# Replacing the per-block interleave of two work threads by one order over all blocks, in a hybrid SSM/RG-LRU decoder layer

## What is computed

```python
h = rms_norm(x, g_mix)
z = h @ w_in + b_in                       # 3584 columns: u_a 512, u_b 1024, two gates of 1024
y_a = s5_mixer(u_a, ...)                  # in projection, complex scan over L, out projection, gelu, GLU
y_b = rglru_mixer(u_b, ...)               # conv of width 4, two sigmoid gates, scan over L
merged = gate_a * (y_a @ w_a_out) + gate_b * (y_b @ w_b_out)
x = x + merged @ w_o
h2 = rms_norm(x, g_ffn)
x = x + (silu(h2 @ w_ffn_gate) * (h2 @ w_ffn_up)) @ w_ffn_down      # hidden 2816
gate_p = sigmoid(rms_norm(x, g_ple_gate) @ w_ple_gate + b_ple_gate)
x = x + gate_p * rms_norm(p @ w_ple, g_ple)
return rms_norm(x, g_final)
```

## Time and profile before

| what | us |
|---|---|
| median of 2 runs | 2377.64 (2377.08 to 2378.2) |
| the profiled execution's own time | 2382.28 |
| its span on the slowest core, 3 | 2380.6 |
| spans of the 8 cores | 2360.8 to 2380.6 |
| PE busy | 1295.1 (54%), 4896 matmuls |
| DVE busy | 1396.3 (59%) |
| ACT busy | 716.3 (30%) |
| chain that ended last | DVE 33%, PE 30%, issue 15%, ACT 12%, DMA 9% |

### The profile page before, as it was taken

How to read it: one execution, slowest core, us unless ns; L and a number is a source line. 1 busy time by engine, 2 the same in 40 slices (tenths; PEclk the granted TensorE clock), 3 DMA queues, 4 the chain that set the end, 5 groups by cost and what they waited for, 6 DMA issues and landing times.

```text
span 2380.6 us, 18703 instructions; the slowest of 8 cores (2360.8 to 2380.6 us)
## 1 busy us (share of the span) xinstructions
PE 1295.1 (54%) x4896; PEld 512.0 (22%) x4896; DVE 1396.3 (59%) x2787; ACT 716.3 (30%) x1085; POOL 143.0 (6%) x153
## 2 busy tenths in 40 slices
PE   0041111256666775356667765267567774388975
PEld 0020000022222321132222321132122221133431
DVE  2608787814777776525877775516777775433123
ACT  0152222061123334361123334351224234312114
POOL 1000000000000100000000100000000100001100
PEclk9995555578879986678879986678779976588987
DMA  9130000036645880435634960425725951348990
GB/s 179 26 72 0 0 0 0 8 80 86 81 58 69 87 108 18 85 79 84 91 51 62 103 92 18 111 57 80 106 36 78 100 79 38 78 62 132 126 106 36
DMA packets 211064, 164.42 MB, mean 69 GB/s; under 512 B 93712, under 2 KB 202896, under 8 KB 210704
## 3 DMA queue, kind: packets, MB, share of 16 engines
q0 software_dynamic: 200928, 132.13, 42.6%
q1 hardware_dynamic: 10032, 31.09, 3.9%
HBM read 286.94 MB, written 8.39 MB: 124 GB/s over the span
## 4 chain that ended last, share of the span: by engine, by line
DVE 33%; PE 30%; issue 15%; ACT 12%; DMA 9%; DVEq 1%; ACTq 0%; SPq 0%; POOL 0%; POOLq 0%
PE ps L452 18%; PE ps L761 4%; DMA slot<-w_b_out 3%; DVE tmp L593 2%; DVE tmp L594 2%; DVE tmp L573 2%; DVE tmp L571 2%; DVE tmp L569 2%; DVE tmp L540 1%; DMA out<-tmp 1%; PE ps L814 1%; DVE tmp L445 1%; DMA slot<-w_in 1%; DVE FB L447 1%; DMA x_fm<-iota 1%
## 5 line engine op out<-in xcount | busy, mean ns | idle before, releaser
L452 PE MATMUL ps<-FB,slot 128*128 128x512 bf16 x1920 | 498.8, 414 | 112.3 <-DVE hid L749 54.5
L452 PEld LDWEIGHTS ps<-FB,slot 128*128 128x128 bf16 x1920 | 196.6, 104 | 399.5 <-issue 218.2
L761 PE MATMUL ps<-hid,slot 128*128 128x512 bf16 x704 | 169.4, 401 | 14.2 <-DMA slot<-w_ffn_down 6.9
L528 PE MATMUL ps<-xcb,wr_sb 128*128 128x512 bf16 x32 | 16.6, 520 | 255.4 <-DVE xcb L525 255.4
L452 PE MATMUL ps<-hid,slot 128*128 128x512 bf16 x384 | 105.3, 423 | 72.2 <-DMA slot<-w_a_out 32.7
L486 PE MATMUL ps<-ident_bf,A 128*128 128x128 bf16 x128 | 16.2, 306 | 212.2 <-DVE small L475 123.8
L612 PE MATMUL ps<-sbf,Csb 128*32 128x512 bf16 x64 | 29.9, 467 | 175.1 <-DVE sbf L605 175.1
L749 DVE TENSOR_TENSOR hid<-tmp,ps 128x512 bf16<-128x512 f32 x88 | 58.8, 685 | 110.3 <-PE ps L452 96.7
L814 PE MATMUL ps<-slot,FB 128*128 128x512 bf16 x256 | 97.1, 523 | 40.7 <-ACT tmp L802 30.5
L445 DVE RECIPROCAL tmp<-tmp 128x512 f32<-128x512 f32 x12 | 40.2, 3353 | 105.8 <-ACT tmp L444 105.8
L452 PE MATMUL ps<-tmp,slot 128*128 128x512 bf16 x384 | 95.4, 413 | 11.4 <-DMA slot<-w_in 10.8
(11 more groups left out here) (203 smaller groups left out, 2421.1 us busy)
## 6 DMA issues: line engine op xcount, KB each, us to landing
slot<-w_in POOLq DMA_DIRECT2D x28, 1024.0 KB, 12.3
slot<-w_ffn_down POOLq DMA_DIRECT2D x32, 704.0 KB, 13.3
slot<-w_ffn_gate POOLq DMA_DIRECT2D x20, 1024.0 KB, 14.5
slot<-w_ffn_up POOLq DMA_DIRECT2D x20, 1024.0 KB, 10.8
tmp<-x SPq DMA_DIRECT2D x32, 512.0 KB, 4.6
slot<-w_b_out POOLq DMA_DIRECT2D x8, 1024.0 KB, 13.9
slot<-w_o POOLq DMA_DIRECT2D x8, 1024.0 KB, 16.0
slot<-w_ple_gate POOLq DMA_DIRECT2D x8, 1024.0 KB, 12.1
```

What stands on the lines that cost most here:

```text
L452: V("pe", lambda e, k=k: e.matmul(ps[:, bn, :], lhsT=slab_lhsT(si, cols, k, c0), rhs=rhs_fn(k), start=(k == 0), stop=(k == kt - 1)), [B_sl ...
L761: V("pe", lambda e, k=k, si=si, cols=cols, bn=bn: e.matmul(ps[:, bn, :], lhsT=slab_lhsT(si, cols, k, 0), rhs=hid[:, k * TB:(k + 1) * TB], ...
```

## The change

A single `schedule` takes two generators that run over all blocks: `S_all` emits S(0) to S(3) one after another, `F_all` emits F(0) to F(3), and F(b) gives way ("W") until S(b) is complete. The next step goes to the side whose position (block number plus the share of its total) is smaller; while the flag `ramp` is set, F and S take turns. The flag is set at the start of each S block and cleared when its RG-LRU and S5 parts begin. The conditions `merged` and `down` stay as they are. The number of steps, their instructions, the weights and the buffers are unchanged.

```diff
+                prog["ramp"] = False
                 gL, gS5 = LRU_gen(), S5_gen()
...
-            run_all(S_thread(0))
-            for b in range(NB):
-                if b + 1 < NB and PIPELINE:
-                    interleave(F_thread(b), S_thread(b + 1), 330.0, 430.0)
-                else:
+            def S_all():
+                for b in range(NB):
+                    prog["ramp"] = True
+                    yield from S_thread(b)
+                    prog["s_done"] = b
+                    prog["s_blk"] = b + 1
+
+            def F_all():
+                for b in range(NB):
+                    while prog["s_done"] < b:
+                        yield "W"
+                    prog["f_blk"] = b
+                    yield from F_thread(b)
+                prog["f_blk"] = NB
+
+            def schedule(gF, gS, totF, totS):
...
+                    if prog["f_blk"] != bF_seen:
+                        bF_seen, pF = prog["f_blk"], 0.0
+                    if prog["s_blk"] != bS_seen:
+                        bS_seen, pS = prog["s_blk"], 0.0
+                    posF = bF_seen + pF / totF
+                    posS = bS_seen - 1 + pS / totS
+                    if doneS or s_blocked:
+                        pickF = True
+                    elif doneF or f_blocked:
+                        pickF = False
+                    elif prog["ramp"]:
+                        turn ^= 1
+                        pickF = bool(turn)
+                    else:
+                        pickF = posF <= posS
...
+            prog.update({"s_done": -1, "s_blk": 0, "f_blk": 0, "ramp": True})
+            if PIPELINE:
+                schedule(F_all(), S_all(), 330.0, 430.0)
```

More of the change, by code:

```diff
@@ new lines, in schedule @@
+            def schedule(gF, gS, totF, totS):
+                pF = pS = 0.0
+                bF_seen, bS_seen = 0, 0
+                doneF = doneS = False
+                f_blocked = s_blocked = False
+                turn = 0
+                while not (doneF and doneS):
+                    if prog["f_blk"] != bF_seen:
[13 more added lines that the diff above has]
+                        pickF = posF <= posS
+                    assert not (pickF and doneF), "scheduler deadlock"
+                    if pickF:
+                        s_blocked = False
+                        try:
+                            c_ = next(gF)
+                            if c_ == "W":
+                                assert not doneS and not s_blocked
+                                f_blocked = True
+                            else:
+                                pF += c_ or 1.0
+                        except StopIteration:
+                            doneF = True
+                    else:
+                        f_blocked = False
+                        try:
+                            c_ = next(gS)
+                            if c_ == "W":
+                                assert not doneF
+                                s_blocked = True
+                            else:
+                                pS += c_ or 1.0
+                        except StopIteration:
+                            doneS = True
@@ L875, in program @@
+            prog.update({"s_done": -1, "s_blk": 0, "f_blk": 0, "ramp": True})
+            if PIPELINE:
+                schedule(F_all(), S_all(), 330.0, 430.0)
+            else:
+                for b in range(NB):
+                    run_all(S_thread(b))
+                    prog["s_done"] = b
                     run_all(F_thread(b))
-                    if b + 1 < NB:
-                        run_all(S_thread(b + 1))
             em.final_wait("sp", B_out + dbg_bufs)
```

## The result

The changed kernel is slower by 0.9%. Its median is 2400.81 us (11 runs, 2394.97 to 2415.0) against 2378.06 us of the kernel before (10 runs beside them); the ratio is 1.0093 with a 95% interval of 1.0074 to 1.0111. That is outside the predicted range of 2357 to 2392, and within the 2% that a measurement was said to tell from no change. A second set of runs beside another 35 runs of before gave 1.0055 (1.0027 to 1.0083). In some executions of the experiments the cores of one half of the chip, or of both, show a lower granted clock and take longer: ratios and means over cores leave these executions out, the medians in the table of the experiments hold them, and e5's only profile is of one.

The account below looks back on a forecast made before the run. No engine fills a block; a long series of small handovers bounds it. Terms 3.2 + 1.3 - 2.7 - 1.7 - 3.8 - 2.2 + 0 + 1.3 = -4.6 us take the median from 2377.64 to 2373.0 us; range 2357 to 2392.

Parts of the forecast that it names:

- Feed-forward part: Feed-forward steps: L749's six waits could shrink or repeat; zero, with 8 us either way for block 1, 2 per other block.
- Start of a block: Three block starts: F's x0 evictions move between S's x0 and x1, lengthening the chain; +3.2 us.
- mg5 beside mg6: Block 1 merge: DVE waits 2.4 us for PE at mg6, a 1.11 us wait at mg5 goes; +1.3 us.
- w_o: w_o steps: scan steps moved ahead cover the first L719 waits; -2.7 us in block 1, -1.7 in blocks 2 and 3.
- Norm and gu0: Block 1 behind w_o: waits for the norm, gu0 and L1a's gates fall from 13.1 to 9.3 us; -3.8 us.
- ple: Block 1's ple steps: ple2's wait grows by 2.5 us, ple3's falls by 4.65; together -2.2 us.
- Table loads: ACT's queue: one more load of a function set than before, at 1.28 us; +1.3 us.
- Late x load: Block starts: F's x0 load lands 4.6 us late, three times; +13.8 us, 2386.8; chance 0.17.
- Finer mixing: Block 1: L749's 11.6 us of waits go and the norm's bound holds; 2357.2 us; chance 0.11.
- overlap after all: S(2)'s and S(3)'s x steps run beside F's tail, hiding 36.5 us each, 73 in all; 2300.0 us; chance 0.02.

Follow-up runs that it names:

- e5: The changed kernel with state 11's a step moved ahead of the dn matmuls it waited for: 2389.24 us, ratio 1.0015 to before.
- e2: The kernel before with state 11's a step moved behind dn2 in each of the three overlapped blocks: 2400.33 us, ratio 1.0035 to before.
- e8: The changed kernel run again, unaltered, on another chip: 2399.66 us, ratio 1.0055 to before.
- e9: The changed kernel with the two input matmuls of each scan state issued one step earlier: 2388.31 us, ratio 1.0027 to before.
- e1: The kernel before with S's x0 step ahead of F's x0 step in the three overlapped blocks: 2387.79 us, ratio 0.9992 to before.
- e7: The kernel before with only the winning exchanges (w_o part, ple3 behind 5_15a) in all three blocks: 2364.74 us, ratio 0.9928 to before.
- e3: The kernel before with block 1 alone in the changed kernel's order: 2396.21 us, ratio 1.0029 to before.
- e4: The kernel before with blocks 2 and 3 alone in the changed kernel's order: 2390.88 us, ratio 1.0002 to before.
- e10: e7 with the input matmuls of each scan state issued one step earlier: 2362.66 us, ratio 0.9931 to before.

## Why the prediction was wrong

The bound was read rightly: a long series of small handovers in which an order matters only where it moves a filler. The step that failed is the list of exchanges, with its zero for the feed-forward part. The text took up those at the block start, the merge, w_o, the norm, gu0 and ple, and gave all the rest to "Feed-forward part ... I take zero, with 8 us either way for block 1 and 2 for each other block". That zero stood on the waits of L749 alone. L749 did stay: its waits moved by no more than 1.2 us in any block on the mean core. But the a step of state 11 changed places with L5a and dn2, so that DVE now reaches it while 22 matmuls of dn stand ahead of its input, and waits 3.3, 5.5 and 4.2 us in the three blocks. The exchange of blocks 2 and 3, made alone and in all three blocks, costs 9.1 +- 2.6 us (e2); taking the step out from behind those matmuls gives back 12.8 of the 15.8 (e5 against e8), and issuing its inputs early 14.2 (e9 against e8, each against before). The section on the change had named "four single steps" in blocks 2 and 3 that change places, and the sum never asked which. The 2 us allowed for each of these blocks could not hold a wait of 5.5. A second part was missed in block 1: the terms that were costed gave -4.6 us in all, but that block grew by 10.6 us on the mean core, of which state 11 is 3.3.

Point by point:

- **Start of a block, +3.2.** Right in its place, wrong in the sum: each L477 behind F's x0 waits 1.0 us longer (4.76 to 5.73), and the slab waits fall by as much and more. e1 measures -1.3 +- 5.1. The prediction costed the slab sequence at nothing and did not draw the consequence: that work put ahead of a slab wait is hidden by it.
- **mg5 beside mg6, +1.3.** Right in its place, mis-sized. The predicted wait of 2.4 was 0.72 + 4.52 = 5.2 in the rows above, and L706 waits 3.2 us more on the mean core. I took PE's 4.5 us from rows at the upper clock level; after 5.34 us of idle, PE ran at the lower (granted clock 0.50). From 613.89 to 617.30 are 3.41 us for eight matmuls, 426 ns each, and from 603.27 to 605.00 in the same kernel 216 ns. The Trainium skill, "TensorE: Matmul & The Clock Gate", Wait — 56ns, not 53.3ns?, gives 426.7 and 215.7 ns between 512-column matmuls at 1.2 and 2.4 GHz; the trace agrees.
- **w_o, -2.7 and -1.7.** The first wait (0.84) goes in all blocks. The second (1.87) stays in block 1, and the last L720 before the norm there waits 0.9 us on the mean core where it waited for nothing, so in block 1 w_o gained nothing at all. It was tied to "the second L719", but it belongs to whichever w_o step stands behind L0a's gates, where PE comes from an idle spell (eight matmuls at 649.64 in 3.62 us). What was not foreseen is that the norm's wait behind w_o falls from 4.5 to 2.5 us in blocks 2 and 3, where one w_o step fewer is left behind 5_4a.
- **Norm and gu0, -3.8.** Predicted 3.6 + 2.8 + 2.9 = 9.3 us of waits; measured 5.61 + 1.07 + 2.90 = 9.6, against 13.1. The sum came out right by luck, two errors cancel. The norm waits 2.0 us more: the way from the last L720 to L445 is 9.6 us, not 7.6, since L537's table load stands in it, which I had costed in a term of its own, and the squares come in pairs every 1.45 us, paced by PE's L441. L568 waits 1.7 less: gu0's matmuls take 7.3 us (679.59 to 686.91), not 8.57. (The terms given for the way to L445 add up to 7.5, not to the 7.6 of the text.) ACT of the kernel after at this norm:

```profile
666.08 1.28 ACT L537 ACT_TABLE_LOAD   x1 [14.04 <-DVE tmp L536]
667.37 0.72 ACT L537 ACTIVATE tmp<-tmp,small 128x512 f32<-128x512 f32 x1
668.00 1.13 ACT L440 ACTIVATE sqb<-x_fm 128x512 bf16<-128x512 f32 x2
669.55 1.15 ACT L440 ACTIVATE sqb<-x_fm 128x512 bf16<-128x512 f32 x2 [0.42 <-PE ps L441]
```

- **ple, -2.2.** ple2 waits 3.82 (3.89 predicted), ple3 1.42 (1.42). But rms3 and ple0, which also changed neighbours, went from 2.45 + 1.36 + 0.97 + 0.30 to 3.73 + 2.00 + 2.49 us, +3.1, and took the gain back. That exchange was not costed either. DVE of the kernel after:

```profile
901.21 3.35 DVE L445 RECIPROCAL tmp<-tmp 128x512 f32<-128x512 f32 x1 [3.73 <-ACT tmp L444]
...
916.01 0.15 DVE L807 TENSOR_SCALAR small<-small 128x1 f32<-128x1 f32 x1 [2.00 <-ACT tmp L806]
...
920.07 0.69 DVE L823 SCALAR_TENSOR_TENSOR tmp<-tmp 128x512 f32<-128x512 f32 x1 [2.49 <-ACT tmp L817]
...
955.84 0.15 DVE L807 TENSOR_SCALAR small<-small 128x1 f32<-128x1 f32 x1 [3.82 <-ACT tmp L806]
...
988.77 0.15 DVE L807 TENSOR_SCALAR small<-small 128x1 f32<-128x1 f32 x1 [1.42 <-ACT tmp L806]
```

- **Table loads, +1.3.** Miscounted. The three changes that the text names are there, but one load less stands ahead of L749 as well: 135 loads before and 135 after. The count does not grow; what mattered is where a load stands, as at the norm above.
- **Late x load (rival).** Did not happen. PE of the kernel after runs F's transposes (L678) right behind S's (L486), with no wait for a load:

```profile
1026.30 1.01 PE L486 MATMUL ps<-ident_bf,A 128*128 128x128 bf16 x8 [8.36 <-ACT A L480]
1027.11 1.91 PE L678 MATMUL ps<-ident_sb,tmp 128*128 128x128 f32 x8
```

- **Finer mixing, and overlap after all (rivals).** The two shares of 0.834 and 0.877 held: no overlap came about. The price named for the overlap, 36.5 us at each border, assumed that four x steps hide in the tail. In the one form that was tried, made from whole steps, nothing of it was found: the two borders turn e7's gain of 19.8 us into a loss of 8.6.

What stays open: over the first set of runs the median grew by 22.7 us, over the second by 15.7, while the mean core grew by about 16 both times (2370.4 in the one profiled execution of before, 2387.0 over twelve of after; then +15.8 +- 2.0). In the first set the slowest core added some 6 us more than the mean. The kernel after scatters more there, 2395 to 2415 against 2377 to 2379 but for one run. No run separates a cause for that. Nor do the parts add up: e3 and e4 give 10.4 by the mean core where e8 gives 15.8, and the interval of about 4 on the difference does not cover that.

## What to carry to other kernels

When a change reorders work in in-order queues, list every pair that changed places, the smallest ones too, and ask of each which operand comes late now. A consumer whose tiny input matmul moves behind a long matmul group waits for it, and so does one that keeps its place behind the group but loses the step that covered it. Here it was cheapest to issue such inputs a step earlier, after which the order matters much less (e9: 15.8 to 1.6 us). In an order that covers its inputs already, early issue brought nothing (e10), and what paid was to keep only the exchanges that put long work ahead of a long wait (e7: 0.7% faster than before).

## What was not expected of the hardware

- An idle spell can cost twice, which a sum from rows at the upper clock level misses: behind 1.31 us of idle eight matmuls took 1.89 us, behind 5.34 us 3.62, and 22 matmuls took 4.92 or, behind 3.71 and 1.04 us of idle with one matmul between them, 7.64. The granted clock over those stretches was 1.00 (1363 to 1371 us) and 0.59 (1371 to 1376). The length of the idle alone does not say how much: before, the same 3.71 us ahead of L528 is followed by a clock of 0.50 from 1361 to 1364 us and of 1.00 from 1365 on, and dn2's and dn3's 44 matmuls take 10.94; after, it is 0.50 from 1372 to 1378. What makes the difference is open.
- Two chains of short operations through ACT and DVE, the x step with its 7.9 us and the ple step with its 15.3 to 15.9, took 25 to 27 us together when they were alternated step by step in the same in-order queues: one after the other and more.
